# Expert stage: rows scattered with their modulation, low halves of all weight units made on VectorE

## The reference, cut to what matters

```python
x = _layer_norm(DN_ALPHA * x + g1 * mix, ln1_g[l], ln1_b[l])
h = _layer_norm(x) * (1.0 + sc2) + sh2             # h: what the experts read
scores = sigmoid(t @ w_router)                     # t: the 512 rows of h, 16 experts
sel = scores + router_bias                         # best group of 4 experts, top 2 in it
gate = top_s / sum(top_s)
hg = t @ w_gate[e]; hu = t @ w_up[e]               # 1024 x 256 each
y += gate_e * ((silu(hg) * hu) @ w_down[e])        # 256 x 1024
x = _layer_norm(DN_ALPHA * x + g2 * ffn, ln2_g[l], ln2_b[l])
```

## Time and profile before

| | us |
|---|---|
| median of 3 runs (3770.85 to 3775.89) | 3772.83 |
| the profiled execution's own time | 3756.39 |
| its span in the trace | 3754.6 |

### The profile page before, as it was taken

The page is one execution under the profiler, slowest core; times in us unless marked ns, Lnnn a source line. Parts: engine busy times, 40 slices in busy tenths (PEclk is TensorE's granted clock), DMA queues, the critical chain, the costliest instruction groups (busy, mean ns, idle before and its releaser), DMA issues. The chain is left out here.

```text
span 3754.6 us, 41065 instructions
## 1 busy us (share of the span) xinstructions
PE 3218.8 (86%) x14735; PEld 2557.3 (68%) x14735; DVE 2410.4 (64%) x3794; ACT 1278.0 (34%) x2024; POOL 573.3 (15%) x147
## 2 busy tenths in 40 slices
PE   4999977886699896788579789678999898989999
PEld 4767756664576685666467568566887687767887
DVE  6756575997676657699743746467765474564445
ACT  2323324764323333467321624232111322231111
POOL 0000001343000000243200000102443000004443
PEclk9999987998799998899779789888999899869999
DMA  7643535997654452799652034013442262102222
GB/s 257 220 166 109 198 98 186 338 334 261 207 177 163 150 171 85 249 335 338 232 199 86 23 99 133 27 62 107 135 155 91 101 189 94 64 23 90 91 99 79
DMA packets 289979, 583.95 MB, mean 156 GB/s; under 512 B 26233, under 2 KB 134209, under 8 KB 282748
## 3 DMA queue, kind: packets, MB, share of 16 engines
q1 hardware_dynamic: 277416, 537.87, 42.8%
q10 hardware_dynamic: 7764, 26.85, 1.8%
q0 software_dynamic: 4608, 16.78, 1.2%
HBM read 529.46 MB, written 78.71 MB: 162 GB/s over the span
## 5 line engine op out<-in xcount | busy, mean ns | idle before, releaser
L132 ACT CAST w_hi<-ring 128x2048 fp32r<-128x2048 f32 (+2 forms) x166 | 308.0, 1858 | 1210.2 <-PE ps L283 1031.1
L283 PE MATMUL ps<-hT_hi,w_hi 128*128 128x512 f32 (+1 forms) x1256 | 499.5, 398 | 26.4 <-DVEq L1117 12.5
L283 PE MATMUL ps<-hT_lo,w_hi 128*128 128x512 f32 (+1 forms) x1256 | 497.3, 396 | 0.0
L139 POOL TENSOR_TENSOR w_lo<-ring,w_hi 128x2048 fp32r<-128x2048 f32 x64 | 307.0, 4798 | 1022.2 <-ACTq L2778 636.8
L144 DVE TENSOR_TENSOR w_lo<-ring,w_hi 128x2048 fp32r<-128x2048 f32 (+3 forms) x112 | 245.4, 2195 | 240.5 <-ACT w_hi L132 240.2
L283 PE MATMUL ps<-hT_hi,w_lo 128*128 128x512 f32 (+1 forms) x1256 | 306.9, 396 | 7.1 <-DVE w_lo L144 7.1
L283 PEld LDWEIGHTS ps<-hT_hi,w_hi 128*128 128x128 f32 (+1 forms) x1256 | 238.1, 190 | 86.5 <-DVEq L1117 14.1
L283 PEld LDWEIGHTS ps<-hT_hi,w_lo 128*128 128x128 f32 (+1 forms) x1256 | 237.0, 189 | 64.6 <-DVE w_lo L144 8.8
L1054 DVE SCALAR_TENSOR_TENSOR piece_sums<-pieces,cond,piece_sums 128x512 f32<-128x512 f32 x294 | 220.8, 751 | 87.6 <-DMA pieces<-in_w_ada_dram 55.5
L283 PEld LDWEIGHTS ps<-hT_lo,w_hi 128*128 128x128 f32 (+1 forms) x1256 | 237.8, 189 | 55.3
L283 PE MATMUL ps<-w_hi,hT_hi 128*128 128x512 f32 (+1 forms) x672 | 259.9, 389 | 1.0 <-ACT w_hi L132 1.0
(11 more groups left out here) (590 smaller groups left out, 6568.1 us busy)
## 6 DMA issues: line engine op xcount, KB each, us to landing
ring<-in_mlp_w_dram SPq DMA_DIRECT2D x64, 1024.0 KB, 5.2
pieces<-in_w_ada_dram SPq DMA_DIRECT2D x96, 512.0 KB, 5.8
ring<-in_w_in_dram SPq DMA_DIRECT2D x36, 1024.0 KB, 7.1
pieces<-in_mod_w_dram SPq DMA_DIRECT2D x72, 512.0 KB, 5.0
raw_sep<-in_w_exp_gate_dram SPq DMA_DIRECT2D x50, 512.0 KB
raw_sep<-in_w_exp_up_dram SPq DMA_DIRECT2D x50, 512.0 KB
raw_sep<-in_w_exp_down_dram SPq DMA_DIRECT2D x24, 1024.0 KB
ring<-in_e_w_in_dram SPq DMA_DIRECT2D x24, 1024.0 KB, 5.5
```

Of the source, the lines that this page charges most:

```text
L132: self.k.nc.scalar.copy(self.k.parts[0][:, i, 0:words], self.k.ring[:, i, 0:words]).then_inc(self.high, 1)
L139: self.k.nc.gpsimd.tensor_tensor(self.k.parts[1][:, i, 0:words], self.k.ring[:, i, 0:words], self.k.parts[0][:, i, 0:words].bitcast(F32), ...
L283: mm = pe.matmul(out, a if weight_left else b, b if weight_left else a, start=first and part == 0 and q == ks[0] and o == 0, stop=last and ...
```

## The change

1. **Rows are scattered modulated.** PE transposes the finished features `hT` back into rows: for each tile t of 128 rows and each of 8 groups of 128 features two matmuls, high and low half against an identity in fp32r, `ident_r` (`rows_back`). ACT copies each tile from its two banks over `xn` (`row_tile`), and POOL waits for that copy, tile by tile.
2. **The modulation of blocks goes.** `exact`, `x_exact`, `mod_pk` and its two DMAs through `scratch` are gone. ACT copies the transposed block from PSUM straight to `xT_hi` in one instruction (`features_high`), and DVE subtracts it from PSUM to give `xT_lo`, one instruction where there were two. PE's next transposes wait for DVE's (`xs_done`), no longer for ACT's (`ex_done`).
3. **All low halves of units go to DVE.** B's is made between `aT_lo` and C's. POOL keeps the scatter and the gather.
4. The warm-up has 80 matmuls where it had 100.

```diff
-        sp.dma_start(cols.rearrange("(j p) -> p j", p=P), k.mod[:, 24:40], allow_slow_non_contiguous=True).then_inc(self.pk_landed, 16)
-        sp.wait_ge(self.pk_landed, 16)
-        sp.dma_start(self.pk[:], cols.rearrange("(i p k) -> p i k", i=2, k=KD)).then_inc(self.pk_landed, 16)
...
+        features = lambda ap: ap[:].rearrange("p (b q) n -> p b (q n)", b=2)
+        back_banks = lambda t: k.ps[:, 5:7, :] if t % 2 == 0 else k.ps[:, 0:2, :]
...
+                pool.wait_ge(x_rows_out, t + 1)
                 for i in range(2):
                     nc.gpsimd.indirect_dma_start(k.slots_x, bass.IndirectOffsetOnAxis(rows[:, i, t:t + 1], 0), xn[:, t, :], None).then_inc(scattered, 16)
-            for b in range(2, NB):
-                s = U.place["B", b]
-                pool.wait_ge(high, s + 1)
-                if s >= PARTS:
-                    pool.wait_ge(unit_read, s - PARTS + 1)
-                nc.gpsimd.tensor_tensor(part(1, s), raw(s), part(0, s).bitcast(F32), ALU.subtract).then_inc(low_pool, 1)
...
+            def rows_back(t):
+                if t >= 2:
+                    pe.wait_ge(x_rows_out, t - 1)
+                for q in range(KD):
+                    o = back_banks(t)[:, q // 4, (q % 4) * P:(q % 4 + 1) * P]
+                    for a in range(2):
+                        mm = pe.matmul(o, hT[a][:, q, t * P:(t + 1) * P], ident_r[:], start=a == 0, stop=a == 1)
+                mm.then_inc(back, 1)
+
+            pe.wait_ge(ident_done, 1)
+            rows_back(0)
+            rows_back(1)
+            rows_back(2)
             pe.wait_ge(mask_done, 1)
...
-            warm_up(k, pe, 7, 100)
+            rows_back(3)
+            warm_up(k, pe, 7, 80)
...
-                for q in range(KD):
-                    last = nc.scalar.activation(ex[:, q, :], k.ps[:, 2 + q // 4, (q % 4) * P:(q % 4 + 1) * P], ACT.Identity,
-                                                scale=pk[:, 1, q:q + 1], bias=pk[:, 0, q:q + 1])
+                nc.scalar.copy(features(xT[b % 2][0]), k.ps[:, 2:4, :]).then_inc(xh_done, 1)
+
+            def row_tile(t):
+                act.wait_ge(back, t + 1)
+                nc.scalar.copy(xn[:, t, :].rearrange("p (b n) -> p b n", b=2), back_banks(t)).then_inc(x_rows_out, 1)
...
-            for s in range(EARLY):
+            row_tile(0)
+            split_high(0)
+            row_tile(1)
+            split_high(1)
+            row_tile(2)
+            row_tile(3)
+            for s in range(2, EARLY):
...
-                link(V.tensor_copy(hi[:], ex[:]))
-                V.tensor_tensor(lo[:], ex[:], hi[:].bitcast(F32), ALU.subtract).then_inc(xs_done, 1)
+                V.tensor_tensor(features(lo), k.ps[:, 2:4, :], features(hi).bitcast(F32), ALU.subtract).then_inc(xs_done, 1)
...
+                if b + 1 < NB and U.place["B", b + 1] >= EARLY:
+                    split_low(U.place["B", b + 1])
                 if b < NB:
                     if U.place["C", b] >= EARLY:
                         split_low(U.place["C", b])
```

More of the change, by code:

```diff
@@ L1120 @@
 class Router:
-    NAMES = "router_landed pk_landed w_split"
+    NAMES = "router_landed w_split"
     def __init__(self, k, c):
@@ L1131, in __init__ @@
         self.steps, self.first_of, self.tri = sb("steps", [P, STEPS]), sb("first_of", [P, N_EXP, N_EXP]), sb("tri_sb", [P, P])
-        self.pk = sb("mod_pk", [P, 2, KD])
     def signals(self, sems):
-        self.landed, self.pk_landed, self.w_split = sems
+        self.landed, self.w_split = sems
     def load(self, sp):
         k = self.k
-        cols = k.scratch[0:2 * D]
         sp.dma_start(self.wr[:], k.A["w_router"].rearrange("(k p) e -> p k e", p=P)).then_inc(self.landed, 16)
@@ L1956, in read @@
         return self.place[kind, b] + 1
[L1958 to L1962, removed]
     def slot(self, s):
@@ L1985, in moe @@
         sb = lambda n, s, t=F32: c.enter_context(nc.sbuf_tensor(fresh(n), s, t))
-        rb, before, first_of, tri, pk = router.rb, router.before, router.first_of, router.tri, router.pk
+        rb, before, first_of, tri = router.rb, router.before, router.first_of, router.tri
         more_rows, overflow, first_row, to_overflow = (router.steps[:, a:b] for a, b in ((0, 3), (3, 10), (10, 26), (26, 42)))
-        ones = sb("ones_r", [P, P])
+        ones, ident_r = sb("ones_r", [P, P]), sb("ident_r", [P, P], F32R)
         sc, sT = sb("sc_r", [P, NT, N_EXP]), sb("sT_r", [N_EXP, S])
@@ L2014, in part @@
             return hT[a][:, 4 * (q - 2):4 * (q - 1), :].rearrange("p k n -> p (k n)") if q < 4 else more[a][:, q - 4, :]
+        features = lambda ap: ap[:].rearrange("p (b q) n -> p b (q n)", b=2)
+        back_banks = lambda t: k.ps[:, 5:7, :] if t % 2 == 0 else k.ps[:, 0:2, :]
         gu = lambda a, s, kk: part(a, s).rearrange("p (g k n) -> p g k n", g=2, k=4)[:, :, kk, :]
-        (block, ones_done, score, score_t, mask_done, ranked, rows_done, of_done,
-         raw0, raw1, raw2, raw3, x0_landed, x1_landed, high, low_dve, low_pool, unit_read, t_done, ex_done, xs_done,
+        (block, ones_done, ident_done, score, score_t, mask_done, ranked, rows_done, of_done,
+         raw0, raw1, raw2, raw3, x0_landed, x1_landed, high, low_dve, unit_read, t_done, xh_done, xs_done, back, x_rows_out,
          sg_done, act_done, at_done, ah_done, al_done, y_done, y0_stored, y1_stored, step) = c.enter_context(
-            stage(nc, "ones_done score score_t mask_done ranked rows_done of_done "
-                      "raw0 raw1 raw2 raw3 x0_landed x1_landed high low_dve low_pool unit_read t_done ex_done xs_done "
+            stage(nc, "ones_done ident_done score score_t mask_done ranked rows_done of_done "
+                      "raw0 raw1 raw2 raw3 x0_landed x1_landed high low_dve unit_read t_done xh_done xs_done back x_rows_out "
                       "sg_done act_done at_done ah_done al_done y_done y0_stored y1_stored step"))
@@ L2167, in split_high, with features_high @@
                 nc.scalar.copy(part(0, s), raw(s)).then_inc(high, 1)
[L2169 removed]
+            def features_high(b):
                 act.wait_ge(t_done, b + 1)
[L2171 to L2179 removed]
+                if b >= 2:
+                    act.wait_ge(unit_read, U.read("B", b - 2))
+                nc.scalar.copy(features(xT[b % 2][0]), k.ps[:, 2:4, :]).then_inc(xh_done, 1)
+            def row_tile(t):
+                act.wait_ge(back, t + 1)
+                nc.scalar.copy(xn[:, t, :].rearrange("p (b n) -> p b n", b=2), back_banks(t)).then_inc(x_rows_out, 1)
+            nc.scalar.activation(sT[:], k.ps[0:N_EXP, 0, :], ACT.Sigmoid).then_inc(score, 1)
+            row_tile(0)
[5 more added lines that the diff above has]
+            for s in range(2, EARLY):
                 split_high(s)
[L2181 removed]
+            features_high(0)
             for b in range(NB + 1):
@@ L2184, in _ @@
                 if b + 1 < NB:
-                    exact(b + 1)
+                    features_high(b + 1)
                     if U.place["A", b + 1] >= EARLY:
@@ L2212, in _ @@
             V.memset(ones[:], 1.0).then_inc(ones_done, 1)
+            V.tensor_copy(ident_r[:], k.ident[:]).then_inc(ident_done, 1)
             dve.wait_ge(score_t, 1)
```

15 lines of the change are left out of this document (5 added, 10 removed).

## The result

The changed kernel takes 3680.62 us (median of 3 runs, 3679.84 to 3683.48) against 3772.83 before: ratio 0.9769, 95% interval 0.9746 to 0.9793, 92 us less. The forecast was 3746, and the lower end of its range 3716. The direction was right and the size was not. 37 more runs of the kernel before, on four chips, lie between 3750.1 and 3776.3 us, most of them under 3770 (one more, in the slow state at a lower granted clock, took 5736.97 and is left out); of the miss of 65 us, 16 are therefore the difference that I carried from the profiled execution (3756.39) to three high runs, and some 50 are in the working. The profiled execution after took 3680.62.

The account below looks back on a forecast made before the run. Engines, with DVE fullest, set the pace and loads barely kept up; after the change loads would bind. Terms 0 - 3.0 - 7.3 - 3.0 = -13.3 us per layer, -27 for two, gave 3730, plus 16.4 carried: 3746 us, range 3716 to 3769.

Parts of the forecast that it names:

- The stretch: Block loop, 20 blocks in 246 us per layer: loads become the bound at 344 GB/s, 238.7 us, a gain of 7.3.
- a rival of 0.13: Block loop: deeper queues let loads run at 376 GB/s throughout, 27.4 + 6 us less per layer, 3706 us; chance 0.13.
- 246 us at 334 against it: Block loop: the argument against much faster loads, one window at 376 GB/s against the whole stretch at 334.
- My upper bound: Block loop: 82.2 MB at the best window's 376 GB/s take 218.6 us, a gain of at most 27.4.
- waits of ACT on landings: Block loop: expected sign of the forecast, ACT waiting for weights to land, absent in the kernel before.
- the first load: Start of the block loop: unit 10's load at 653.86 comes earlier, 3.0 us gained per layer, bounds 0.6 and 4.
- the tail: Last weights issued to last result, 17.6 us: one long low half goes, 3.0 us gained per layer, bounds 0 and 6.
- the 7.0 us from the first transposes to the first product: Start of the block loop, 628.18 to 635.14: two times the transposes, 2.91, 0.68 and 1.2; forecast to become 6.4 us.
- The start: Row matmuls between transposed scores and rank matmuls: value 0 us, bounds a gain of 0.7 and a loss of 17.
- the cover: Serial start: the 5.4 us in which DVE makes the mask, 587.7 to 593.1, meant to hide 48 row matmuls.
- The sign I had set myself: Serial start: the forecast is wrong there if the row numbers come after 606; expected at 603 or a little before.
- The carried difference: Whole kernel: runs' median 3772.8 lies 16.4 us above the profiled execution's 3756.4, added to 3730 to give 3746.

Follow-up runs that it names:

- less work: Kernel after with three quarters of the low-half pass of A and B left out from block 2 on, same transfers: 3674.82 us, ratio 0.9752.
- 1.2% and 1.0% alone: Kernel before with all low halves on DVE only: 3722.81 us, 0.9884; kernel after with B's low halves given back to POOL: 3722.94 us, 0.9896.
- with units 2 and 3 between the copies: Kernel after with one tile of row matmuls ahead of the ranks, and ACT making high halves of units 2 and 3 between tile copies: 3672.62 us, 0.9754.

## Why the prediction was wrong

**The stretch: the failed step.** "I take it that they then run at 0.99 of the engines' time ... in place of 0.96, at the same bytes per busy time" took the DMA share for a load factor and so sized the term at 7.3 us; it measured 37.3 for 18 blocks, which is 41 for 20. The run with extra work on DVE shows 0.97 at 348 GB/s, the kernel after 1.02 at 401: bytes per busy time are not constant. (A transfer in flight may count as busy however slowly it moves; no run shows that.) The working had the evidence against itself: engines set the pace, said the waits, and then the gain of engines is not lost to loads unless something shows a limit. PE's 10.2 us per block, the next limit by the prediction's own numbers, gives 20 x (12.3 - 10.2) = 42 us, where 41 came; so near a hit would have been partly luck, as PE's work came to 9.8 and a block to 10.4. Windows at 376 GB/s showed that 344 was none; I kept this as a bound and as a rival of 0.13, and "246 us at 334 against it" was no evidence, as loads that follow engines show their pace. My upper bound, 27.4 us at 376, was too low for the same reason, and because I took the best window of the stretch for the best of the trace. Windows of the kernel before, one far ahead of the stage and one in its start, show more:

```profile
20.00:30.00 10.00, 0.00 (x0) 0.00 (x0) 9.57 (x15) 0.00 (x0) 0.00 (x0) 1.00 1.05 394
...
610.00:620.00 10.00, 10.00 (x92) 10.00 (x91) 5.92 (x9) 3.08 (x2) 6.63 (x5) 1.00 1.00 393
```

At 393 GB/s the 82.2 MB take 209 us, a gain of 37.

The Trainium skill's figure for a core (DMA: Bandwidth & Descriptors, section "Where 436 GB/s comes from", about 358 GB/s) is no ceiling here: 401 over 180 us, 412 with less work.

**What was right.** The direction; that engines bound before and not loads, and why DVE was so full (low halves of 5.2 to 5.5 us beside POOL's: POOL reading does it, POOL writing does not); DVE's work after (9.7 forecast, 193.47 / 207 x 10.41 = 9.7); 2.29 us for all low halves; waits of ACT on landings; the first load and the tail, -4.4 and -3.6 where I had -3.0 each. PE and ACT came out at 9.8 and 7.3 us (10.2 and 6.9 forecast), the former at a clock of 1.00 in place of 0.94. One reading was loose: the 7.0 us from the first transposes to the first product are not the sum given for them, which makes 8.7. The path is 1.97, then ACT's 2.91, then PE's second transposes, 1.94; DVE's part runs beside these. It came to 6.0 (634.36 to 640.38), forecast 6.4.

**The start: the second failed step.** 48 matmuls at 0.12, "5.8 us, 0.4 over the cover", were 48 at 0.213, 10.2 us, and 10.2 - 5.4 = 4.8 over the cover: +4.9 us measured, not 0. The price came from a row at 2.4 GHz and was used in a stretch whose own rank matmuls I had just read as running at 1.2; the row at 256 columns times two would have given 0.24 and a delay of 6.1. I also let PE's work raise the clock; it stayed at 0.50 through all of it. The sign I had set myself (row numbers after 606) came. The loss hid under the larger gain.

**The carried difference.** 16 us from one execution to a median of three were the spread of runs (3750 to 3776), not an offset.

## What to carry to other kernels

A DMA share near 1 does not prove that loads bind; ask who waits for landings, and if nobody does, cost a faster engine at the engines' next limit and keep the loads' limit as a rival, at the highest rate that any window of the trace shows. Two parts of a change that shorten work in the same loop can add up in full: here 1.2% and 1.0% alone, 2.2 to 2.3% together. Take a matmul's price at the clock of the stretch in which it will run.

## What the runs showed of the hardware

- One core's loads and stores ran at 401 GB/s for 180 us and at 412 for 150 us; a DMA share of 0.95 to 1.02 stood beside anything from 334 to 412 GB/s.
- A DVE subtraction of 128x2048 with both inputs in SBUF takes 2.29 us alone or beside POOL's settings of a tensor, 3.0 to 3.8 in the mean beside POOL's subtractions.
- An fp32r matmul of 128 columns with its own weights costs 0.11 us at 2.4 GHz and 0.21 at 1.2, hardly less than one of 256 (0.12): below 256 columns there was nothing to save.
- An indirect DMA's issue on POOL takes 0.95 to 1.15 us, and 1.9 to 2.7 beside a two-input subtraction of DVE; one that began together with the subtraction took 0.95 (with units 2 and 3 between the copies), and beside `x_res`'s scaling by a constant the issues stayed at 0.95 to 1.15. In the kernel after:

```profile
610.89 0.96 POOL L2058 DMA_INDIRECT slots_x<-ring,rows_r  x1 [0.30 <-issue]
612.16 2.66 POOL L2058 DMA_INDIRECT slots_x<-ring,rows_r  x1 [0.30 <-issue]
615.13 1.89 POOL L2058 DMA_INDIRECT slots_x<-ring,rows_r  x1 [0.30 <-issue]
```
